# Inverting the 128x128 triangles of a delta-rule scan as 64x64 quarters, with the two halves of each level placed around halves of a projection unit

## The reference

```python
def step(S, inp):
    r_t, w_t, k_t, v_t, kk_t, a_t = inp
    sa = jnp.einsum('bhvk,bhk->bhv', S, -kk_t)
    S = S * w_t[:, :, None, :] + sa[..., None] * (kk_t * a_t)[:, :, None, :] + v_t[..., None] * k_t[:, :, None, :]
    return S, jnp.einsum('bhvk,bhk->bhv', S, r_t)
```

## Time and profile before

| | |
|---|---|
| median of 3 runs | 1887.74 us |
| the profiled execution | 1885.17 us |
| its span | 1883.4 us |
| TensorE (PE) busy | 1731.8 us, 92% of the span |
| VectorE (DVE) busy | 1368.5 us, 73% |
| ScalarE (ACT) busy | 1002.6 us, 53% |
| TensorE's clock granted, mean | 0.969 of full |
| lines 590, 596 and 505 on the triangles, busy | 46.9, 48.2 and 31.3 us |

### The profile page before, as it was taken

How to read it: one execution, slowest core, us unless ns; L and a number is a source line. 1 busy time by engine, 2 the same in 40 slices (tenths; PEclk the granted TensorE clock), 3 DMA queues, 4 the chain that set the end, 5 groups by cost and what they waited for, 6 DMA issues and landing times.

```text
span 1883.4 us, 27888 instructions
## 1 busy us (share of the span) xinstructions
PE 1731.8 (92%) x10784; PEld 1532.1 (81%) x10784; DVE 1368.5 (73%) x1242; ACT 1002.6 (53%) x919; POOL 31.1 (2%) x20
## 2 busy tenths in 40 slices
PE   6898998879999789899989599999999999999996
PEld 6797897868999679888888488888888888888885
DVE  5757755675444676766475688989898988888887
ACT  4363243633333344523344376767676776767674
POOL 0000000001000200000000100000000000000000
PEclk9899999998999799999999799999999999999998
DMA  8322322464665343223234598989999999999993
GB/s 262 114 91 90 112 86 91 136 179 134 178 178 178 122 147 112 90 88 93 68 121 168 190 351 321 374 318 379 330 374 331 356 337 360 331 362 354 342 364 121
DMA packets 252061, 411.29 MB, mean 218 GB/s; under 512 B 8400, under 2 KB 133840, under 8 KB 251344
## 3 DMA queue, kind: packets, MB, share of 16 engines
q1 hardware_dynamic: 249440, 400.68, 61.6%
q10 hardware_dynamic: 2544, 9.54, 1.4%
HBM read 408.09 MB, written 2.10 MB: 218 GB/s over the span
## 4 chain that ended last, share of the span: by engine, by line
PE 78%; DVE 14%; ACT 4%; issue 4%; DMA 1%; SPq 0%; DVEq 0%; ACTq 0%
PE W L428 16%; PE W L430 16%; PE W L429 16%; PE Y L428 5%; PE Y L429 5%; PE Y L430 5%; PE Y L596 2%; PE Y L590 2%; PE Y L785 2%; ACT w_hi L952 2%; DVE w_lo L1330 2%; PE W L505 1%; DVE sc L1475 1%; PE Y L505 1%; DVE xt L1492 1%
## 5 line engine op out<-in xcount | busy, mean ns | idle before, releaser
L428 PE MATMUL W<-w_lo,x_hi 128*128 128x512 f32 (+1 forms) x1120 | 393.0, 351 | 9.1 <-DVE x_lo L1629 6.5
L430 PE MATMUL W<-w_hi,x_hi 128*128 128x512 f32 (+1 forms) x1120 | 387.6, 346 | 0.0
L429 PE MATMUL W<-w_hi,x_lo 128*128 128x512 f32 (+1 forms) x1120 | 386.9, 345 | 0.0
L1330 DVE TENSOR_TENSOR w_lo<-raw,w_hi 128x2048 fp32r<-128x2048 f32 x115 | 263.2, 2292 | 165.7 <-ACT w_hi L952 164.6
L1337 DVE TENSOR_TENSOR w_lo<-raw,w_hi 128x2048 fp32r<-128x2048 f32 x144 | 329.7, 2290 | 52.5 <-ACT w_hi L958 52.3
L958 ACT ACTIVATE w_hi<-raw 128x2048 fp32r<-128x2048 f32 x144 | 276.0, 1917 | 83.3 <-PE Y L430 43.7
L428 PE MATMUL W<-x_lo,w_hi 128*128 128x256 f32 x992 | 294.2, 297 | 22.1 <-DVE w_lo L1330 15.7
L1337 DVE TENSOR_TENSOR w_lo<-raw_more,w_hi 128x2048 fp32r<-128x2048 f32 x120 | 275.0, 2291 | 32.0 <-ACT w_hi L958 31.9
L429 PE MATMUL W<-x_hi,w_lo 128*128 128x256 f32 x992 | 285.7, 288 | 0.0
L430 PE MATMUL W<-x_hi,w_hi 128*128 128x256 f32 x992 | 285.4, 288 | 0.0
L958 ACT ACTIVATE w_hi<-raw_more 128x2048 fp32r<-128x2048 f32 x120 | 230.7, 1922 | 67.1 <-PE W L430 43.9
(11 more groups left out here) (278 smaller groups left out, 2097.7 us busy)
## 6 DMA issues: line engine op xcount, KB each, us to landing
raw<-w_in SPq DMA_DIRECT2D x124, 512.0 KB, 4.7
raw<-moe_gate SPq DMA_DIRECT2D x48, 1024.0 KB, 7.0
raw<-moe_up SPq DMA_DIRECT2D x48, 1024.0 KB, 7.7
raw<-moe_down SPq DMA_DIRECT2D x48, 1024.0 KB, 6.2
raw_more<-moe_gate SPq DMA_DIRECT2D x40, 1024.0 KB, 7.5
raw_more<-moe_up SPq DMA_DIRECT2D x40, 1024.0 KB, 7.3
raw_more<-moe_down SPq DMA_DIRECT2D x40, 1024.0 KB, 6.9
raw<-w_branch SPq DMA_DIRECT2D x24, 512.0 KB, 4.4
```

Of the source, the lines that this page charges most:

```text
L428: nc.tensor.matmul(out_ap, lhs[0], rhs[1], start=start, stop=False)
L429: nc.tensor.matmul(out_ap, lhs[1], rhs[0], start=False, stop=False)
L430: return nc.tensor.matmul(out_ap, lhs[0], rhs[0], start=False, stop=stop)
L1330: V.tensor_tensor(w_lo[u % 3][:], raw[u % 3][:], w_hi[u % 3][:].bitcast(F32), ALU.subtract)\
```

## The change

The triangle is taken as two 64x64 quarters on its diagonal and one below. The two diagonal quarters are kept compactly: `ac`, `mc`, `xn` (the inverse) and `xt[:, :, 0]` (its transpose) hold 64 numbers a partition for each of the 8 triangles, the first quarter in partitions 0 to 63, the second in 64 to 127. Levels 1 to 5 work on these alone, with matmuls of 64 rows by 64 columns (`blocks`): 16 for `mx`, and 32 for `dx`, since both `xt` and `xn` are now carried along (8 transposes a level go away). The masks are made compact once at the start, on GpSimd (`cm`). Level 6 makes the remaining quarter with 8 matmuls in `mx` and 8 in `dx`. In `chain`, the product with the inverse becomes two matmuls for a head (64 rows by 64 columns, then 128 rows by 64 columns). ScalarE copies the two diagonal quarters into `ac` after the scores.

A projection unit can be done in two parts: `front` is its first output tile (24 matmuls) and the split of unit u+2, `back` its second tile and the emptying of the bank. A level is `mx` between the two and `dx` behind. Level 6 of pass 1, which followed level 5 directly, now has the unit `gate1` 2 around it, which stood behind `finish` before, and the unit `gate1` 1 no longer stands between level 6 and `chain`.

```diff
-    ("ss", 1), ("knorm", 1), ("units", "gate0", 0, 1), ("kk", 1), ("level", 0, 4),
-    ("units", "gate0", 1, 2), ("prep", 1), ("level", 0, 5),
-    ("conv", 0), ("units", "gate0", 2, 3), ("level", 0, 6),
+    ("ss", 1), ("knorm", 1), ("front", "gate0", 0), ("kk", 1), ("mx", 0, 4), ("back", "gate0", 0), ("dx", 0, 4),
+    ("front", "gate0", 1), ("prep", 1), ("mx", 0, 5), ("back", "gate0", 1), ("dx", 0, 5),
+    ("conv", 0), ("front", "gate0", 2), ("mx", 0, 6), ("back", "gate0", 2), ("dx", 0, 6),
...
-    ("units", "qkv", 3, 4), ("rope", 1), ("level", 1, 2),
-    ("units", "qkv", 4, 5), ("rope", 2), ("level", 1, 3),
-    ("units", "qkv", 5, 6), ("rope", 3), ("level", 1, 4),
-    ("units", "gate1", 0, 1), ("level", 1, 5), ("level", 1, 6),
-    ("units", "gate1", 1, 2), ("chain", 1, 0), ("chain", 1, 1), ("finish", 1),
-    ("units", "gate1", 2, 4), ("osplit", 1), ("heads",), ("units", "branch1", 0, 2),
+    ("front", "qkv", 3), ("mx", 1, 1), ("back", "qkv", 3), ("dx", 1, 1), ("rope", 1),
+    ("front", "qkv", 4), ("mx", 1, 2), ("back", "qkv", 4), ("dx", 1, 2), ("rope", 2),
+    ("front", "qkv", 5), ("mx", 1, 3), ("back", "qkv", 5), ("dx", 1, 3), ("rope", 3),
+    ("front", "gate1", 0), ("mx", 1, 4), ("back", "gate1", 0), ("dx", 1, 4),
+    ("front", "gate1", 1), ("mx", 1, 5), ("back", "gate1", 1), ("dx", 1, 5),
+    ("front", "gate1", 2), ("mx", 1, 6), ("back", "gate1", 2), ("dx", 1, 6),
+    ("chain", 1, 0), ("chain", 1, 1), ("finish", 1),
+    ("units", "gate1", 3, 4), ("osplit", 1), ("heads",), ("units", "branch1", 0, 2),
...
+            def blocks(bank, left, right):
+
+                for u in range(8):
+                    for half in HALVES:
+                        last = nc.tensor.matmul(tiles(bank[:], 8)[half, u, :], left(half, u), right(half, u), start=True, stop=True)
+                return last
...
+            def mx(l, p, v):
+
+                n = 2 * l + p
+                if v == 1:
+                    pe.wait_ge(sem("x0_ready"), n + 1)
+                else:
+                    pe.wait_ge(sem("x_ready"), 5 * n + v - 1)
+                if v < TOP:
+                    pe.wait_ge(sem("mc_ready"), 5 * n + v)
+                    last = blocks(Y[0], lambda half, u: mc[half, u, :], lambda half, u: xn[half, u, :])
...
+            def dx(l, p, v):
+
+                n = 2 * l + p
+                pe.wait_ge(sem("mx_ready"), TOP * n + v)
+                if v < TOP:
+                    blocks(Y[1], lambda half, u: mc[half, u, :], lambda half, u: xt[half, u, 0, :])
+                    last = blocks(Y[2], lambda half, u: xt[half, u, 0, :], lambda half, u: mc[half, u, :])
...
-                    last = nc.tensor.matmul(Y[1][:, hc], xt[:, 4 * c + h, :], g_s[:, h, :], start=True, stop=True)
+                    nc.tensor.matmul(Y[1][0:HD, hc], xt[0:HD, 4 * c + h, 0, :], g_s[0:HD, h, :], start=True, stop=True)
+                    last = nc.tensor.matmul(Y[1][HD:P, hc], xt[:, 4 * c + h, 1, :], g_s[:, h, :], start=True, stop=True)
...
+            def mx(l, p, v):
+                n = 2 * l + p
+                if v == TOP:
+                    act.wait_ge(sem("x_ready"), 5 * n + 5)
+                    A(xt[HD:P, :, 1, :], xt[HD:P, :, 0, :], ACT.Copy).then_inc(sem("column_ready"), 1)
+                act.wait_ge(sem("mx_done"), TOP * n + v)
+                rows = slice(HD if v == TOP else 0, P)
+                A(mc[rows], tiles(Y[0][:], 8)[rows], ACT.Copy).then_inc(sem("mx_ready"), 1)
...
+            def dx(l, p, v):
+                n = 2 * l + p
+                dve.wait_ge(sem("dx_done"), TOP * n + v)
+                if v == TOP:
+                    mark(V.tensor_copy(xt[0:HD, :, 1, :], tiles(Y[1][:], 8)[0:HD]), "corner_ready", n + 1)
+                    return
+                V.tensor_tensor(xt[:, :, 0, :], xt[:, :, 0, :], tiles(Y[1][:], 8), ALU.add)
+                mark(V.tensor_tensor(xn[:], xn[:], tiles(Y[2][:], 8), ALU.add), "x_ready", 5 * n + v)
+                if v < TOP - 1:
+                    mask_level(n, v + 1)
```

More of the change, by code:

```diff
@@ L443, in x_part, with proj_unit @@
                     pe.wait_ge(sem("x_lo_ready"), 4 * m + k // 2 + 1)
-            def proj_unit(u, j, fresh=None):
-                i = 0
-                unit_ready(u, i)
-                bank = job_bank(j, i)
+            def proj_unit(u, j, fresh=None, parts=(0, 1)):
+                if 0 in parts:
+                    unit_ready(u)
+                    job_bank(j)
+                bank = tiles(W[j % 3][:])
                 wh, wl = (w[u % 3][:].rearrange("p (k c) -> p k c", k=KD) for w in (w_hi, w_lo))
-                for m in range(2):
+                for m in parts:
                     c = slice(m * P, (m + 1) * P)
@@ L457, in proj_unit, with front, back @@
                                    k == 0, k == KD - 1)
-                last.then_inc(w_used, 1)
+                if 1 in parts:
+                    last.then_inc(w_used, 1)
+            def front(l, kind, q):
+                proj_unit(layer_unit(l) + UNIT0[kind] + q, l * MIX_JOBS + JOB0[kind] + q, parts=(0,))
+            def back(l, kind, q):
+                proj_unit(layer_unit(l) + UNIT0[kind] + q, l * MIX_JOBS + JOB0[kind] + q, parts=(1,))
             def branch_unit(l, b, u, j):
@@ new lines, in mx @@
+            def mx(l, p, v):
[7 more added lines that the diff above has]
+                    last = blocks(Y[0], lambda half, u: mc[half, u, :], lambda half, u: xn[half, u, :])
+                else:
+                    for u in range(8):
+                        last = nc.tensor.matmul(tiles(Y[0][:], 8)[HD:P, u, :], sc[0:HD, u, 0, HD:P], xn[0:HD, u, :],
+                                                start=True, stop=True)
+                last.then_inc(sem("mx_done"), 1)
@@ new lines, in dx @@
+            def dx(l, p, v):
[4 more added lines that the diff above has]
+                    last = blocks(Y[2], lambda half, u: xt[half, u, 0, :], lambda half, u: mc[half, u, :])
+                else:
+                    for u in range(8):
+                        last = nc.tensor.matmul(tiles(Y[1][:], 8)[0:HD, u, :], mc[HD:P, u, :], xt[HD:P, u, 0, :],
@@ L597, in level @@
                                                 start=True, stop=True)
[L598 to L600 removed]
+                last.then_inc(sem("dx_done"), 1)
             def chain(l, p, c):
@@ L904, in _ @@
             handlers = {"units": units, "lora_w": lora_w, "lora_a": lora_a, "ss": ss, "tok": tok, "scores": scores, "invert": invert,
-                        "level": level, "chain": chain, "finish": finish, "rope": rope, "heads": heads, "att_scores": att_scores,
+                        "front": front, "back": back, "mx": mx, "dx": dx, "chain": chain, "finish": finish, "rope": rope, "heads": heads, "att_scores": att_scores,
                         "probs_t": probs_t, "att_out": att_out}
@@ L1347, in units, with front @@
                         gate_unit(l, int(kind[-1]), q, u0 + q, j0 + 2 * q)
+            def front(l, kind, q):
+                split_lo(layer_unit(l) + UNIT0[kind] + q + 2)
             def gate_unit(l, b, q, u, j):
@@ L1826, in _ @@
             handlers = {"units": units, "shift": shift, "conv": conv, "decay": decay, "ksq": ksq, "kk": kk, "prep": prep,
-                        "decayed": decayed, "bonus": bonus, "scores": scores, "invert": invert, "level": level, "chain": chain,
-                        "finish": finish, "rope": rope, "att_scores": att_scores, "softmax": softmax,
+                        "decayed": decayed, "bonus": bonus, "scores": scores, "invert": invert, "dx": dx, "chain": chain,
+                        "front": front, "finish": finish, "rope": rope, "att_scores": att_scores, "softmax": softmax,
                         "att_out": att_out, "osplit": osplit, "msplit": msplit}
```

122 lines of the change are left out of this document (55 added, 67 removed).

## The result

The changed kernel takes 1895.68 us (median of 11 runs, 1890.94 to 1899.69); the kernel before, beside it, 1888.21 us (11 runs). The ratio is 1.0037, with an interval of 1.0023 to 1.0051: 0.4% slower, inside what I had called the same, and outside my range of 1838 to 1872. The profiled execution took 1898.07 us (span 1896.3), so 49.9 us are missing against the 1848.2 of the sum.

The account below looks back on a forecast made before the run. TensorE's time bounds the inversion's levels; gains of 13.1 us (pass 0) and 9.4 us (pass 1), twice, less 8 us in `chain`, make 37 us: 1848.2 from 1885.2, median forecast 1851 us, range 1838 to 1872.

Parts of the forecast that it names:

- the sum: Whole kernel: gains of both passes, counted for two layers, less the cost in `chain`: 37 us off 1885.2, giving 1848.2.
- the copies into `ac` that were put at nothing: Ahead of `invert`: ScalarE's two copies lie under the last unit and cost no time.
- the sixth unit: Pass 1: a unit that stood later (5.84 us) moves into the inversion, so 63.5 us before is counted as 69.3.
- the full clock that the sum assumed throughout: All stages: TensorE's instructions were priced at its full clock, 2.4 GHz.
- The price of a small matmul: Inversion: diagonal pairs run side by side, 28 ns an instruction; 55 ns if they do not.
- Rival 1: Inversion: the quarters don't run side by side, 55 ns an instruction, +56 us in all, 1907 us; chance 10%.
- A level, pass 0 and pass 1: Inversion: a level of pass 1 every 10.1 us instead of 11.75, pass 0 in 59 us, pass 1 in 60.
- Rival 3: Pass 0: VectorE or ScalarE binds, the second part's 7.3 us gain is lost twice, 1866 us; chance 8%.
- The cost in chain: `chain`: eight products with the inverse take 2.1 us instead of 1.10, +1.0 for each of 8 calls, 8 us.
- The price of a shape change: TensorE: about 0.1 us at each border, 0.38 us for each block of small matmuls between units.
- Rival 2: `chain`: TensorE's clock falls, some 2 us of products a call at half clock, +16 us, 1867 us; chance 12%.

Follow-up runs that it names:

- e1: Changed kernel with ScalarE's copies into `ac` moved behind its split of the weights: 1881.33 us, ratio 0.9946 to the kernel before.
- e11: Changed kernel with the units of pass 1 put back where they stood before the change: 1887.14 us, ratio 0.9986 to the kernel before.
- e10: Changed kernel's order of work around half units, but with the old inversion on 128x128 numbers: 1908.35 us, ratio 1.0099 to the kernel before.
- e3: Changed kernel with both the edit of e1 and that of e2: 1864.76 us, ratio 0.9864 to the kernel before.
- e4: e3 plus 64 unread products in the waits of `chain`, behind g and behind u: 1851.09 us, ratio 0.9805 to the kernel before.
- e2: Changed kernel with the products in `chain` grouped, four of 64x64 first, then four of 128x64: 1883.01 us, ratio 0.9963 to the kernel before.
- e9: e4 plus 54 more unread products a layer, ahead of `chain`, in `finish` and ahead of the heads' transposes: 1842.92 us, ratio 0.9759 to the kernel before.

## Why the prediction was wrong, point by point

Three steps failed: the copies into `ac` that were put at nothing (12.3 us), the sixth unit that was subtracted whole (3.7 us of waits), and the full clock that the sum assumed throughout (some 33 us between the profiled executions, an estimate).

- **The price of a small matmul** (28 ns against 55): right but for 10%, 31 ns start to start inside a block. A block of `mx` with its borders adds 1.27 us to the unit in the timeline, as forecast (0.89 + 0.38). Rival 1, at 10%, is out. Its rule, from the Trainium skill (TensorEngine Tiling (Array Packing), Gotcha 1: PSUM Pressure), that different row tiles cannot access the same PSUM bank at the same time, does not show as a serialisation here: the two halves write one bank, in different partitions, at 31 ns an instruction where one after the other would have been 55.
- **A level, pass 0 and pass 1**: 10.08 us (forecast 10.1) and 58.9 (59.0); pass 1 took 62.4 and 61.3 instead of 60.0, of which the window 228 to 235, with its clock of 0.54, has most; in e1 it took 59.7. Rival 3 (VectorE or ScalarE binds pass 0) is out.
- **"At nothing: ScalarE's two copies into `ac`, under the last unit ahead of `invert`"**: wrong, 12.3 us in the table of stages. I set copies that take 1.27 us against a unit of 5.8, and didn't ask what stands behind the copies in ScalarE's queue. The copies wait 6.3 us for the last triangle, and the split behind them waits too. Nothing of it shows in the length of an instruction.
- **The cost in chain**, +1.0 us a call: right at full clock (2.05 us for eight), but five of the eight calls ran at half clock, where it is 3.2 us. The price of a shape change was right; the clock at which it is paid was not.
- **"The sixth unit stood later (5.84)"**: wrong as a full gain. In its old place the unit covered VectorE's work behind `finish` (+1.44 and +0.4 us of waits in a layer). And a unit that stood ahead of `chain` was moved away with it: with the old order of units e11 has `chain` 6.5 and 5.6 us shorter, though e10 shows that its absence alone needn't lower the clock.
- **Rival 2 (TensorE's clock falls)** is what happened, at 12% and +16 us. The mechanism was the right one and its size was half: I took 2 us a call, in `chain` alone. The windows show the lower clock reaching over `chain` and all of `finish` in pass 1 (0.55 over 22 us), and into the units behind. By the yardstick it is 25 to 33 us. I had seen 0.57 in a stretch of the kernel before and priced it for `chain` alone, though products already ran at the lower clock there and the change made the stage longer.
- At equal clock the changed kernel is 1871 us, and with the queue mended (e1) 1858, 7 above the 1851 that I forecast; the waits behind `finish` are 4 of the 7. That e3 comes to 1850 at equal clock, and e4 to 1851 as measured, is luck: they have grouped shapes or filled waits, which the forecast did not have. The terms for the inversion itself were right.

What stays open: what decides whether the clock falls in `chain` of pass 1 (in e10 it fell in one layer and not in the other, in e2 it rose with no unit ahead), why the clock is also lower in some later stretches of the attention, which the change doesn't touch, and why executions of one kernel differ in it. No run separates these.

## What to carry to other kernels

Price a copy by its place in the queue, not by its length: name what stands behind it on its engine and when its own input comes. When a change makes TensorE's work shorter near a stage of small products and short waits, read the granted clock there first and in every layer, keep dense work directly ahead of the stage, and group products by shape; where nothing else fits into a wait and the clock has fallen, unread products can be worth their time (13.7 us in e3, 4 in the kernel before). And compare kernels at equal clock as well as by their medians, since executions of the kernel before alone lie up to 15 us apart along with their clock.

## What the runs showed of the hardware that I had not expected

- TensorE fell to its 1.2 GHz level in stretches where it was busy for most of the time: 18.29 of 22 us in the chain and `finish` of pass 1, where no single wait in its timeline is over 0.86 us (the busy time is itself longer at the lower clock). In the kernel before, 12 us of the same stage with 9.22 us busy were at full clock, behind a dense unit, and so were 12.5 us with 9.25 busy in layer 1 of e10, with no unit ahead.
- 64 unread products of 128x256 took 13.7 us off e3. With the larger filling of e9 the five executions lay within 3 us, where e4's five lay within 14.
- A change of shape costs 0.1 us more a product when products of 64 and 128 rows alternate (0.25 against 0.15 us), at full clock.
